# Shared block of a hybrid decoder layer: the later tile's chain step ahead of the pair of expert jobs in each beat, on VectorE and ScalarE

## What is computed

```python
# attention: indexer scores, top-k keys, softmax over the chosen keys
s = relu(einsum('bthd,bsd->bths', qi, k_idx) * IDX_DIM ** -0.5); score = einsum('bths,bth->bts', s, wi)
vals, idx = top_k(score, k_sel);  p = softmax(logits + bias);  o = p @ v
# PEER: 8 heads, two lists of 128 keys, top-16 of each, 256 candidates, top-16 again -> 128 experts a token
s1, i1 = top_k(s[:, :, 0], 16); s2, i2 = top_k(s[:, :, 1], 16)
top, pos = top_k(cand, 16);  eid = take_along_axis(cid, pos);  g = softmax(top)
act = gelu(einsum('nhed,nd->nhe', u_tab[eid], x))       # one dot product of 1024 per expert
out = einsum('nhe,nhed->nd', g * act, v_tab[eid])       # and its row of v, weighted
```

## Time and profile before

| what | value |
|---|---|
| time, median of 3 runs | 2857.42 us (2853.36 to 2862.12) |
| the profiled execution's own time | 2862.56 us |
| its span, first to last instruction | 2860.4 us |
| PE busy | 1996.0 us (70%) |
| DVE busy | 1458.1 us (51%) |
| ACT busy | 517.9 us (18%) |
| POOL busy | 718.4 us (25%) |
| DMA | 786.40 MB, mean 275 GB/s |
| matmuls of the experts, L1094 | 752.2 us |
| dot products of the experts, L1443 | 678.4 us |

### The profile page before, as it was taken

The page is one execution under the profiler, slowest core; times in us unless marked ns, Lnnn a source line. Parts: engine busy times, 40 slices in busy tenths (PEclk is TensorE's granted clock), DMA queues, the critical chain, the costliest instruction groups (busy, mean ns, idle before and its releaser), DMA issues.

```text
span 2860.4 us, 25952 instructions
## 1 busy us (share of the span) xinstructions
PE 1996.0 (70%) x8208; PEld 1105.8 (39%) x8208; DVE 1458.1 (51%) x2961; ACT 517.9 (18%) x1812; POOL 718.4 (25%) x609
## 2 busy tenths in 40 slices
PE   7799999996775536775575675577642557768666
PEld 2288887533554413342132431143420112545311
DVE  2000000107643866588684696865763688225554
ACT  0001000001211114222241222232211112102121
POOL 0000000003211033634333434335330224134342
PEclk9899999996766768887787977788975777576789
DMA  8711212103215589999999999989993799889797
GB/s 272 246 59 63 85 59 78 48 8 104 59 57 185 162 324 397 418 398 414 407 356 418 394 419 408 395 354 420 394 376 99 294 380 373 309 337 396 301 421 311
DMA packets 209212, 786.40 MB, mean 275 GB/s; under 512 B 26707, under 2 KB 83891, under 8 KB 139044
## 3 DMA queue, kind: packets, MB, share of 16 engines
q0 software_dynamic: 78976, 572.70, 49.7%
q1 hardware_dynamic: 118550, 191.21, 19.3%
q10 hardware_dynamic: 11552, 20.85, 2.4%
HBM read 764.31 MB, written 22.73 MB: 275 GB/s over the span
## 4 chain that ended last, share of the span: by engine, by line
DMA 24%; DVE 16%; PE 13%; issue 8%; SPq 5%; POOL 2%; ACT 1%; ACTq 1%; DVEq 0%; POOLq 0%
DMA uv<-in_peer_uv,eidr 13%; PE PS L1094 6%; DMA wr<-in_w_oq 5%; DVE uv L1443 3%; PE PS L1174 2%; SPq L995 2%; PE PS L1154 2%; DMA uv<-in_peer_uv,eid 1%; DVE m L1473 1%; SPq L1001 1%; POOL uv L1051 1%; PE PS L1223 1%; DMA kvr<-in_cache_v 1%; DMA gater<-gate_d 1%; DVE sels L1474 1%
## 5 line engine op out<-in xcount | busy, mean ns | idle before, releaser
L1094 PE MATMUL PS<-uv,dg 128*32 128x512 f32 x2176 | 752.2, 770 | 484.1 <-ACT dg L1303 438.9
L1443 DVE CUSTOM_DVE_ANT_0 uv<-uv,h2r 128x1024 f32<-128x1024 f32 x544 | 678.4, 1247 | 494.0 <-DMA uv<-in_peer_uv,eidr 414.0
L1051 POOL DMA_INDIRECT uv<-in_peer_uv,eidr x512 | 581.7, 1136 | 1194.7 <-PE PS L1094 978.8
L1094 PEld LDWEIGHTS PS<-uv,dg 128*32 128x32 f32 x2176 | 202.8, 128 | 904.6 <-ACT dg L1303 593.1
L368 PE MATMUL PS<-hT,wb 128*128 128x272 f32 (+1 forms) x1696 | 390.9, 394 | 17.0 <-PEq L134 17.0
L368 PEld LDWEIGHTS PS<-hT,wb 128*128 128x128 f32 (+1 forms) x1696 | 314.8, 186 | 94.0 <-issue 18.8
L1291 ACT ACTIVATE acts<-dots 128x2 f32<-128x2 f32 x272 | 55.2, 203 | 1197.3 <-DVE dots L1443 1153.2
L1174 PEld LDWEIGHTS PS<-h2T,wr 128*128 128x128 f32 x1280 | 176.1, 221 | 75.9 <-issue 72.6
L1174 PE MATMUL PS<-h2T,wr 128*128 128x128 f32 (+1 forms) x1280 | 188.8, 307 | 9.1 <-DMA wr<-in_w_oq 7.8
L505 POOL DMA_DIRECT2D lbp<-in_lb_param x2 | 1.8, 912 | 637.0 <-POOLq L134 637.0
L1303 ACT ACTIVATE dg<-fold,wts 128x32 f32<-128x32 f32 x544 | 140.8, 305 | 0.0
(11 more groups left out here) (251 smaller groups left out, 1780.6 us busy)
## 6 DMA issues: line engine op xcount, KB each, us to landing
wr<-in_w_oq SPq DMA_DIRECT2D x120, 512.0 KB
wb<-in_w_in SPq DMA_DIRECT2D x15, 2048.0 KB, 7.8
w_ada_b<-in_w_ada SPq DMA_DIRECT2D x12, 2048.0 KB, 8.1
h2r<-h_d ACTq DMA_DIRECT2D x32, 256.0 KB
uv<-in_peer_uv,eidr POOLq DMA_INDIRECT x512
kvr<-in_cache_kt SPq DMA_DIRECT2D x64, 128.0 KB
kvr<-in_cache_v SPq DMA_DIRECT2D x64, 128.0 KB
vec<-mod_d SPq DMA_DIRECT2D x12, 512.0 KB
```

The source lines that it names most:

```text
L1051: nc.gpsimd.indirect_dma_start(out=uv[j % RING][:, :], out_offset=None, in_=table, in_offset=bass.IndirectOffsetOnAxis(ids, 0)).then_inc(e ...
L1094: mm = nc.tensor.matmul(PS[ST * g:ST * g + ST, at:at + 512], dg[:, j % DR, :], uv[j % RING][:, D + 512 * half:D + 512 * half + 512], start ...
L1443: c.step(nc.vector.tensor_tensor_reduce(out=uv[j % RING][:, 0:D], in0=uv[j % RING][:, 0:D], in1=h2r[:, q // HT % 2, g % 2, :], scale=1.0, ...
```

## The change

In every beat, DVE and ACT take their part of the steps first and their part of the pair of jobs second. PE, POOL and SP keep their order. No instruction is added or removed.

```diff
@@ -1422,10 +1422,10 @@
             act.wait_ge(z_in, 16 * 5)
             for q in range(-1, NG + 1):
+                for s in beats[q]:
+                    step(*s)
                 if 0 <= q < NG:
                     activations(q)
-                for s in beats[q]:
-                    step(*s)
```

## The result

| | before | after |
|---|---|---|
| median, us (4 runs each) | 2855.39 (2845.78 to 2862.12) | 2931.09 (2912.7 to 2938.46) |
| span of the profiled execution, us | 2860.4 | 2930.7 |
| PE / DVE / ACT busy, us | 1996.0 / 1458.1 / 517.9 | 2017.4 / 1461.0 / 522.1 |
| mean granted clock, of full speed | 0.809 | 0.811 |
| L1443 / L1094, us | 678.4 / 752.2 | 681.7 / 784.3 |

The change makes the kernel slower: ratio 1.0258, 95% interval 1.0202 to 1.0314. The forecast was 2926 us, in a range of 2878 to 2990. The total is right, and part of that is luck: the terms for the closed rounds were too small, and a gain of about 20 us, which no step of the prediction had, stood against them.

The account below looks back on a forecast made before the run. The block was taken to pass between DMA and DVE as limits, paced by buffer return. Terms 32 + 13 + 18 + 8 + 6 - 8 = +69 us on a median of 2857.4 gave 2926 us, range 2878 to 2990.

Parts of the forecast that it names:

- closed rounds: Each step on DVE comes directly behind the previous pair, so ACT, PE and DVE go in turn, without one pair of slack.
- Attention, +32 forecast: Steps 0 to 3, 12 beats: DVE waits for PE's logits; +32 us, bounds +18 and +55.
- the 0.7 us for the clock: Tile 1's attention round: 28% of values and logits time at the lower clock lifts 8.8 us to 9.5.
- the clock falls with it: Whole kernel: PE, waiting more, gets 1.2 GHz nearly always; near 3090 us, half of it 3000; 8% chance.
- `idx`, +13 forecast: Five beats: round of 9.1 us against some 6 today; +13 us, bounds +5 and +18.
- `query`, +18 forecast: 54 beats, tiles 1 to 3: ACT waits for PE ahead of `acts`, lengthening light beats; +18 us, bounds 0 and +48.
- Sample `query`, +8: Sample tokens' 9 query beats: `acts` then stands behind the last `qT` copy; +8 us, bounds +2 and +14.
- single places, +6: `norm` 0, `smid`, `smax`, `snorm`, `smerge`, `fin` 0: the pair done during DVE's wait comes behind it; +6 us, bounds 0 and +20.
- Given back by `spread`, -8: Tiles 1 and 2: `spread` one pair earlier shortens POOL's waits for `gater`; -8 us, bounds -20 and 0.
- DMA hides it: Whole kernel: slower buffer return only replaces present waits; attention and `idx` terms halve, query and sample vanish; 2879 us; 14% chance.
- Faster: At `spread` and `fin` 0, work moves into DVE's waits for gathers; -20 us, 2840 us; 7% chance.
- Nothing to tell: Whole kernel: steps wait so little that both sides cancel; within 0.3% of 2857 us; 7% chance.

Follow-up runs that it names:

- the rest beats alone: Steps first on DVE and ACT in all beats without an att, query or idx step of tiles 1 to 3, against the kernel before: 2859.92 us, ratio 1.0004.

## Why the prediction was right, step by step

**The round.** Right, and it is most of the result. DVE waits for L1109 as said (13 waits, 4.2 us each in place of the 2 to 3 forecast), the beats of tile 1 behind the first take 10.98, 10.67 and 10.45 us (9 to 12 forecast), and PE's order alone takes the whole loss away.

**Attention, +32 forecast.** Mechanism right, size too small: +45 us measured with those beats alone, within the bounds of +18 and +55 and near the upper one (+36.5 in its stretches with the whole change). The mis-sized term is the 0.7 us for the clock. I took 28% at the lower level, from the 0.86 of the `query` window; the window of the earlier trace rows that holds tile 1's attention has 0.75, which is half the time. Neither would have been enough, since in the new beats the values ran at the lower level nearly always. Windows of L1094 alone in tile 1's attention, before and after:

```profile
1070.00:1097.00 27.00, 10.65 (x37) 1.73 (x33) 0.87 1.01 413
```

```profile
1085.00:1121.00 36.00, 14.22 (x32) 4.30 (x32) 0.74 0.62 235
```

0.29 us a matmul before, 0.44 after; 8 of them are 1.2 us more a round. My 9.5 us with the values at 3.67 and not at the 2.4 us that 28% makes is 10.7, which is the beat measured. In tiles 2 and 3 two of the new beats take 12.76 and 13.35 us, with values of 3.83 and 3.77, where the forecast had 10.8 and 12.0. So the rival "the clock falls with it" was true of the values alone, in these beats and in several `query` beats, where I had priced it as all or nothing; over the whole kernel the clock did not fall (0.811 against 0.809). The drain that the Trainium skill ("ScalarE: Activation LUTs", What ACT_TABLE_LOAD costs) adds to each table load is not in this case's rows: ACT's last copy ends at 1104.93, the load runs from 1104.94 to 1106.22, and the next activation starts at 1106.31.

**`idx`, +13 forecast.** With those beats alone +9 by the ratio and +15 in their own stretches. The round of tile 2's second beat (timeline after; the earlier trace rows before) is 10.90 us from one `acts` to the next, 9.1 forecast, and again the difference is the values, 3.83 us:

```profile
1412.55 0.20 ACT L1291 ACTIVATE acts<-dots 128x2 f32<-128x2 f32 x1 [3.30 <-DVE dots L1443]
...
1413.53 3.83 PE L1094 MATMUL PS<-uv,dg 128*32 128x512 f32 x8 [4.81 <-ACT dg L1303]
...
1418.90 1.27 DVE L1484 SCALAR_TENSOR_TENSOR lg<-rel,kw_s,lg 128x384 f32<-128x384 f32 x2 [6.38 <-ACT rel L1343]
...
1423.45 0.20 ACT L1291 ACTIVATE acts<-dots 128x2 f32<-128x2 f32 x1 [4.03 <-DVE dots L1443]
```

**`query`, +18 forecast.** The size holds roughly (+25.9 in its stretches with the whole change, +18.3 with those beats alone), the place does not. "The heavy beat hides the round, the light one does not" is the step that failed: the light beat stayed at 4.38 us and the heavy one grew from 7.58 to 8.90 or more. I had priced the wait on ACT, ahead of `acts`. It falls on DVE, ahead of the search of the heavy beat, since the light beat ahead is shorter than PE's round and DVE arrives before the copy. The sum of a light and a heavy beat, 13.3 to 14.0 forecast, was 13.3 in the first rows shown and 14.6 to 15.8 in three later pairs of tile 1, whose first has the values at 3.34 us and DVE's wait of 3.01. Of the two other signs, ACT's `acts` follows the pair's dot products in the light beat (1244.07), as before, and its own copy only in the heavy one; and the DMA share of those beats fell only from 1.02 to 0.99.

**Sample `query`, +8, and single places, +6.** The step for the sample tokens said that `acts` is done while PE works today, and would stand behind ACT's last copy afterwards. The first half was read wrongly. In the kernel before, too, `acts` of these beats follows the last copy of `qT`, and DVE waits 9.15 us for it (timeline before):

```profile
2664.28 0.20 ACT L1326 ACTIVATE qT<-PS 128x32 f32<-128x32 f32 x1 [3.92 <-PE PS L1174]
2664.37 0.20 ACT L1291 ACTIVATE acts<-dots 128x2 f32<-128x2 f32 x1
...
2664.69 1.23 DVE L1443 CUSTOM_DVE_ANT_0 uv<-uv,h2r 128x1024 f32<-128x1024 f32 x1 [9.15 <-ACT acts L1291]
```

After the change the same two rows are there, and DVE's wait is 9.34 us. What is new is that PE now waits for `dg`, which before had been made a beat ahead (timeline after):

```profile
2686.87 0.20 ACT L1291 ACTIVATE acts<-dots 128x2 f32<-128x2 f32 x1
...
2687.19 1.23 DVE L1443 CUSTOM_DVE_ANT_0 uv<-uv,h2r 128x1024 f32<-128x1024 f32 x1 [9.34 <-ACT acts L1291]
...
2687.84 3.37 PE L1094 MATMUL PS<-uv,dg 128*32 128x512 f32 x8 [0.54 <-ACT dg L1303]
```

That is 0.53 or 0.54 us in seven of these beats and 1.3 in the two at their start, where I had 0.9 each; the kernel before has no such wait in them. The size of the whole is open. The stretch shows +7.6, and kernels with before's order there show -7 to -9 in it, so it may be +8 or +16. The kernel with all these other beats moved, which holds both terms and the next one, came out at 1.0004 [0.9986, 1.0022]: -4 to +6 us for the three together, where I had 8 + 6 - 8 = +6.

**Given back by `spread`, -8.** POOL's waits for `gater` went as said, and no time went with them: the stretches around `spread` are 3.0 us longer with the rest beats alone. (In that kernel one wait is gone and the other is still 9.25 us.) POOL waits for PE there instead.

**Not in the prediction: the set-up, -21.7.** My text said that steps are priced by the round that they close. It did not ask what a *later release of buffers* does to other users of the DMA engines. The profile before had the sign of it: one issue of 128 KB on SP's queue that took 19.25 us.

**The sum.** +69 was forecast for the profiled execution and +70.3 was measured, of which 5.3 lie ahead of the first gather, where the code is the same. The closed rounds cost about 88 us by the table (8.4 + 36.5 + 17.2 + 25.9) where I had 32 + 13 + 18 = 63; 8.8 were given back behind them and 21.7 in the set-up, and the coarse stretch of the sample tokens adds 7.6. So the total was met by an under-sized loss and an unseen gain of about the same size, and that is luck. The forecast's own range was also added up wrongly: the four bounds named for it give 2894 to 2979, not 2885 to 2985.

**The rivals.** *DMA hides it* holds in small: DVE's waits for gathers fell by 138 us, and of the 95 us of new waits on L1109 and L1332 part only replaced them, but the whole is far from 2879. *Faster* fails as a whole, though a gain of about its price, 20 us, exists at another place than I named. *Nothing to tell* fails. *The clock falls with it* fails as a whole; its two terms, +146 and +55, make 3058 and half of them 2958, not the 3090 and 3000 of the text.

## What to carry to other kernels

Where engines meet once a beat, what counts is how many pairs of work lie between the producer's and the consumer's turn; moving two of three engines takes that slack away, and moving the third restores it, at no change in instructions. Price a closed round with the matmuls behind PE's wait at the lower clock: here they took 3.35 to 3.83 us in tile 1's attention beats, where the earlier trace rows have 1.91. And look for small-packet loads that share the DMA engines with a deep queue of gathers: holding the gathers for 14 us was worth 0.45% here, and a change elsewhere can take or give that without touching it.

## What the runs showed of the hardware

- SP's queue and POOL's take turns packet by packet, whatever the packets' size, while both have work: 265 and 266 packets in 5 us, 0.11 and 1.94 MB. The issue of a 128 KB load in 128-byte packets took SP's queue 19.25 us beside gathers, 1.94 us with fewer of them queued, and 0.67 us with the gathers held.
- In tile 1's attention beats after the change PE waited 4.6 to 5.9 us ahead of each pair's values, and these took 3.35 to 3.83 us, at or near the lower of TensorE's two clock levels; in the kernel with PE's order moved as well, the values of the same beats took 1.91 to 2.96 us.
- A table load of 1.28 us followed ACT's work before it after 0.01 us, and the next activation followed the load after 0.09 us; where the dot products were done earlier (1500.02 to 1500.03) it was 0.01 us.
